# Attention values in runs of up to four steps, with strided sums of the weights on VectorE

## What is computed

```python
s = einsum('bqhd,bkhd->bhqk', q_nope, k_nope) + einsum('bqhr,bkr->bhqk', q_rope, kpe)
p = softmax(s * scale, axis=-1)
o = einsum('bhqk,bkhd->bqhd', p, v)
```

## Time and profile before

| | us |
|---|---|
| median of three runs | 3077.3 (3075.81 to 3077.61) |
| span of the profiled execution, first to last instruction | 3073.1 |
| the profiled execution's own time beside its span | not listed apart; the median lies 4.2 above the span |
| attention, first score to last convolution tile | about 930 to 1836 |

### The profile page before, as it was taken

One profiled execution on the slowest core, in us unless ns is written; L12 is line 12 of the kernel. 1 busy time (PEld: TensorE's weight loads), 2 busy tenths in 40 slices (PEclk: granted clock), 3 DMA queues, 4 the chain that ended last, 5 costly groups with the idle time before them and its releaser, 6 DMA issues. The chain is left out here.

```text
span 3073.1 us, 42659 instructions
## 1 busy us (share of the span) xinstructions
PE 2897.7 (94%) x16288; PEld 2284.8 (74%) x16288; DVE 1953.7 (64%) x2559; ACT 1085.5 (35%) x1723; POOL 1070.6 (35%) x693
## 2 busy tenths in 40 slices
PE   6999999999889999999999999989977999999993
PEld 3888888888676666666666667878856888888882
DVE  5418292829438888888888866555575555555555
ACT  5311111111344444444444443223432333434344
POOL 1000000000105343443433554522136766666652
PEclk9999999999898999999999999999988999999996
DMA  6213222211441110110110117675534666666657
GB/s 235 102 50 108 79 102 79 100 73 61 171 152 32 27 33 7 32 33 7 34 26 6 55 53 226 182 248 179 168 135 140 199 205 200 194 204 211 205 186 291
DMA packets 139518, 371.25 MB, mean 121 GB/s; under 512 B 20886, under 2 KB 47996, under 8 KB 129116
## 3 DMA queue, kind: packets, MB, share of 16 engines
q1 hardware_dynamic: 99756, 266.55, 26.0%
q0 software_dynamic: 24048, 74.72, 8.6%
q10 hardware_dynamic: 15552, 27.79, 2.6%
HBM read 266.07 MB, written 102.89 MB: 120 GB/s over the span
## 5 line engine op out<-in xcount | busy, mean ns | idle before, releaser
L1209 ACT ACTIVATE at_w<-banks 128x512 f32<-128x512 f32 (+1 forms) x592 | 347.6, 591 | 463.6 <-PE banks L1316 407.9
L1432 DVE TENSOR_REDUCE at_mpart<-banks 128x1 f32<-128x512 f32 (+1 forms) x584 | 373.7, 682 | 136.5 <-PE banks L1343 136.5
L1288 POOL TENSOR_TENSOR at_part<-at_part,at_w 128x512 f32<-128x512 f32 x224 | 297.6, 1329 | 327.2 <-ACT at_w L1209 323.9
L2705 POOL TENSOR_TENSOR late<-moe_raw_gu,late 128x2048 fp32r<-128x2048 f32 x62 | 287.2, 4633 | 121.6 <-ACT late L2770 121.3
L536 DVE SCALAR_TENSOR_TENSOR fr_r<-fr_r,fr_dw 128x2334 f32<-128x2334 f32 x120 | 318.0, 2650 | 3.9
L393 PE MATMUL fr_po<-hT_hi,fr_w_hi 128*128 128x512 f32 (+1 forms) x800 | 297.3, 372 | 3.0 <-PE fr_po L393 1.8
L393 PE MATMUL fr_po<-hT_hi,fr_w_lo 128*128 128x512 f32 (+1 forms) x800 | 294.9, 369 | 0.0
L393 PE MATMUL fr_po<-hT_lo,fr_w_hi 128*128 128x512 f32 (+1 forms) x800 | 294.9, 369 | 0.0
L1354 PE MATMUL banks<-at_w,V 128*64 128x256 f32 (+1 forms) x2368 | 283.0, 381 | 0.0
L2897 DVE TENSOR_TENSOR late<-raw,late 128x1024 fp32r<-128x1024 f32 x64 | 192.0, 3001 | 100.8 <-ACT late L2809 100.8
L1458 DVE TENSOR_TENSOR at_part<-at_part,at_w 128x512 f32<-128x512 f32 x224 | 231.5, 1033 | 13.0
(11 more groups left out here) (404 smaller groups left out, 6295.6 us busy)
## 6 DMA issues: line engine op xcount, KB each, us to landing
moe_raw_gu<-w_gate_up SPq DMA_DIRECT2D x62, 1024.0 KB, 4.8
raw<-w_down SPq DMA_DIRECT2D x64, 512.0 KB, 4.0
fr_wm<-w_ada_rows POOLq DMA_DIRECT2D x32, 512.0 KB, 4.3
gates_scratch<-fr_r ACTq DMA_DIRECT2D x64, 256.0 KB, 2.0
mx_gates<-gates_scratch SPq DMA_DIRECT2D x64, 256.0 KB, 3.1
fr_raw<-w_in SPq DMA_DIRECT2D x28, 512.0 KB, 5.5
fr_r<-x POOLq DMA_DIRECT2D x18, 512.0 KB, 5.5
raw<-mixed_scratch SPq DMA_DIRECT2D x9, 1024.0 KB, 6.0
```

The source lines that it names most:

```text
L1209: act.activation(w[:, g % NW, k, 0:n], sc[:, (2 * g + k) % SCB, 0:n], ACT.Exp, scale=SM_SCALE).then_inc(exp_done, 1)
L1288: pool.tensor_tensor(part[:, j % 2, 1, 0:n], before, w[:, g % NW, 1, 0:n], ALU.add).then_inc(add_p, 1)
L1432: dve.tensor_reduce(mpart[:, s, tiles, c // 2], bank, AX.X, ALU.max).then_inc(red_done, 1)
L2705: pool.tensor_tensor(gu_lo[:, slot], raw_gu[:, slot], gu_hi[:, slot].bitcast(F32), ALU.subtract).then_inc(glo_done, 1)
```

## The change

Steps are put into groups by a list of the last step of each (`ENDS`): 0 to 2, 3 to 6, 7 to 10, 11 to 14, 15 to 17, 18 to 21, 22 to 25, 26 to 29, 30 to 33, 34 to 35, and the prompt's step 36 together with 0 to 2 of the next head. For each group TensorE does the scores and maxima of all its steps, then the sums of blocks that ended in the group before, then the values of the same group in one run.

`part` goes; `w` has six slots in its place, the outer two of which hold the partial sums. The steps of a group lie in the inner four so that the steps of one block, with the partial sum so far at their side, are neighbours. VectorE sums them in one `tensor_reduce` that reads the slots with the slot as the innermost dimension (neighbouring elements of a sum are 2 x 512 floats, 4096 bytes, apart) and writes the partial sum on the other side or, for the first and last run of a block, on the block's own side. GpSimd still adds one step at a time. The prompt's sum is made by TensorE from its two tiles with ones, in a bank of the maxima's ring, and no engine adds or copies for it. ScalarE takes finished blocks out after the exponentials of the group that follows. The convolution's pieces keep their step numbers.

```diff
+    ENDS = (2, 6, 10, 14, 17, 21, 25, 29, 33, 35)
...
+    GROUPS = [[]]
     for g in range(G):
-        ADDS.append(ADDS[-1] + joins(g))
+        GROUPS[-1].append(g)
+        if g % PER in ENDS and g + 1 < G:
+            GROUPS.append([])
...
-        w = p.sb("w", [P, NW, 2, BLK])
-        part = p.sb("part", [P, 2, 2, BLK])
+        w = p.sb("w", [P, NW + 2, 2, BLK])
...
-                        if g >= NW:
-                            act.wait_ge(pv_mm, g - NW + 1)
-                            act.wait_ge((add_d, add_p)[k], adds_over(g - NW))
+                        if USED_BY[g] is not None:
+                            act.wait_ge(pv_mm, USED_BY[g] + 1)
+                            if whole(block_of(USED_BY[g])):
+                                act.wait_ge((add_d, add_p)[k], (D_ADDS, P_ADDS)[k][USED_BY[g]])
...
+                    for k in range(2 if own else 0):
+                        for half in range(2):
+                            mm = pe.matmul(acc_of(j)[half * DV:(half + 1) * DV, 256:256 + n], ones[:],
+                                           w[:, SLOT[g], k, half * n:(half + 1) * n],
+                                           start=(k == 0), stop=(k == 1), skip_group_check=True)
...
-                for g in range(0, G, 2):
-                    scores(g)
...
-                    if g:
-                        values(g - 2)
-                        values(g - 1)
...
+                for n, group in enumerate(GROUPS):
+                    for g in group:
+                        scores(g)
+                        for m in maxima_at(g):
                             max_products(m)
-                    if g:
-                        for j in turns(g + LA):
+                        for j in turns_at(g):
                             turn_max(j)
...
+                    for j in summed(n):
+                        sum_up(j)
+                    for g in group:
+                        values(g)
...
-                def add(g):
...
-                        dve.tensor_tensor(part[:, j % 2, 0, 0:n], before, w[:, g % NW, 0, 0:n], ALU.add).then_inc(add_d, 1)
+                def add(j, members):
+                    own = 0 if j % BH % 2 == 0 else NW + 1
+                    other_side = NW + 1 - own
+                    lo, hi = SLOT[members[0]], SLOT[members[-1]]
+                    out = other_side if third(j, members) == 1 else own
+                    dve.wait_ge(exp_done, 2 * members[-1] + 1)
+                    if third(j, members):
+                        dve.wait_ge(add_d, D_ADDS[members[-1]] - 1)
+                        lo, hi = min(lo, NW + 1 - out), max(hi, NW + 1 - out)
+                    if third(j, members) == 1 and number(j):
+                        dve.wait_ge(sum_mm, number(j))
+                    dve.tensor_reduce(w[:, out, 0], w[:, lo:hi + 1, 0].rearrange("p s n -> p n s"), AX.X, ALU.add).then_inc(add_d, 1)
...
+                    for j, members in RUNS[n]:
+                        add(j, members)
+                        if last_of(j) in members:
+                            join(j)
```

More of the change, by code:

```diff
@@ L1000, in turns, with summed, alone, unit_entries @@
         return [j for j in range(1, H * BH) if last_of(j) in (m - 2, m - 1)]
[L1002 to L1006, removed]
+    def summed(n):
+        return [j for j, members in (RUNS[n - 1] if n else ()) if last_of(j) in members]
+    def alone(n):
+        return [g for g in GROUPS[n] if not whole(block_of(g))]
+    def unit_entries(m):
+        return [("unit", UNITS[m] + half) for half in range(halves_of(m))] if m < G else []
+    def maxima_at(g):
+        if g < 2:
+            return (FIRST_MAX + 2 * g, FIRST_MAX + 2 * g + 1)
+        return (g + LA,) if g + LA < G else ()
+    def turns_at(g):
+        return turns(g + LA) if g > 1 and g % 2 == 0 else []
+    RING = [entry for m in range(FIRST_MAX) for entry in unit_entries(m)] + [("turn", 0)]
+    for n, group in enumerate(GROUPS):
+        for g in group:
+            RING += [entry for m in maxima_at(g) for entry in unit_entries(m)] + [("turn", j) for j in turns_at(g)]
+        RING += [("own", block_of(g)) for g in alone(n) if g + 1 < G]
     BANK, BEFORE, LAST_IN = {}, {}, {}
@@ L1082, in bank_of, with acc_of, part @@
             return mx[:, at] if at < MXB else sc[:, at - MXB]
+        def acc_of(j):
+            if whole(j) or last_of(j) + 1 == G:
+                return acc[:, number(j) % 2]
+            return bank_of(("own", j))
+        def part(j, k):
+            return w[:, 0 if j % BH % 2 == 0 else NW + 1, k]
         def paired(m):
@@ L1275, in _ @@
                         fold_conv(g % PER // 2 - 7)
-                    if not joins(g):
+                    j = block_of(g)
+                    if not whole(j) or c == 0:
                         continue
-                    j, n = block_of(g), BLOCKS[b][1]
                     pool.wait_ge(exp_done, 2 * g + 2)
[L1280 to L1288, removed]
+                    if c > 1:
+                        pool.wait_ge(add_p, P_ADDS[g] - 1)
+                    elif before(j) >= 0:
+                        pool.wait_ge(sum_mm, number(before(j)) + 1)
+                    so_far = part(j, 1) if c > 1 else w[:, SLOT[g - 1], 1]
+                    pool.tensor_tensor(part(j, 1), so_far, w[:, SLOT[g], 1], ALU.add).then_inc(add_p, 1)
                 for k in range(CT):
@@ L1322, in bank_free @@
                         kind, n = BEFORE[entry]
-                        pe.wait_ge(red_done if kind == "unit" else row_done, n + 1)
+                        pe.wait_ge({"unit": red_done, "turn": row_done, "own": o_done}[kind], n + 1)
                 def turn_max(j):
@@ L1410, in _ @@
-                values(G - 2)
-                values(G - 1)
-                for j in ended(G - 2) + ended(G):
-                    sum_up(j)
+                        if g == G - PER + TAIL:
+                            pe.wait_ge(conv_const, 2)
+                            pe.wait_ge(c_summed, 3)
+                            pe.wait_ge(row_done, H * BH)
+                            pe.matmul(mean, mean_w, sq[:, 0], start=True, stop=True).then_inc(mean_mm, 1)
+                        if g == G - PER + TAIL + 6:
+                            pe.wait_ge(sq_summed, 3)
+                            pe.matmul(var, mean_w, sq[:, 0], start=True, stop=True).then_inc(var_mm, 1)
```

175 lines of the change are left out of this document (77 added, 98 removed).

## The result

The change makes the kernel slightly slower: 3085.65 us (median of six runs, 3083.49 to 3088.74) against 3076.97 (six runs, 3075.81 to 3077.97), a ratio of 1.003 with a 95% interval of 1.002 to 1.004. The forecast was 3059, so it missed by 27 us and had the wrong sign; 3085.65 lies inside the range, near its upper end. The profiled execution took 3083.59 us, its span is 3081.8.

The account below looks back on a forecast made before the run. TensorE's own stream was taken to bound attention. Terms -25.2 + 1.7 + 0 + 5.4 = -18.1 us took the span from 3073.1 to 3055.0, and with 4.2 for the median 3059 us; range 3050 to 3090.

Parts of the forecast that it names:

- I take 1.04: VectorE's strided sum: 1.04 ns an element at a 4096-byte step, the rate of a contiguous reduction.
- sums by one strided operation: VectorE in attention: 96 reductions replace 256 additions, each ending before TensorE needs the next exponentials; cost 0.
- Bounds and range: Strided sum's rate: lower bound 1.04 ns an element, upper 2.02; whole kernel's range 3050 to 3090 us.
- the limits: Where a late sum stalls TensorE: fourth score tile's exponential by 13.3 us, fourth maxima unit's bank by 14.9.
- The hop is charged: Rival at VectorE's group sum: the wide step slows it and stalls TensorE; +67 us, 3126 us, chance 0.24.
- Fewer runs: TensorE in attention: 74 fewer runs of values at 0.34 us of joints each, -25.2 us.
- Joints not all saved: Rival at TensorE's joints: some gaps remain however values are grouped, a run worth 0.19 us; 3070 us, chance 0.07.
- Sum late though the rate holds: Rival at VectorE's group sum: uncounted waits add 1 us in three groups a head; 3072 us, chance 0.08.
- Prompt by products: TensorE's prompt sum: two more products with ones per head, 0.22 us in each of 8 heads, +1.7 us.
- Order at the end: Last head: the convolution norm's chain through root and silu ends later, delaying the last products; +5.4 us.
- faster: Whole kernel: outcome below 3071 us, faster by over 0.2%, given chance 0.66.

Follow-up runs that it names:

- experiment 1: The kernel before, with the values of each pair of steps split into two runs of one step, 147 more runs: 3129.9 us, ratio 1.017.
- experiment 5: The changed kernel, with strided sums over at most three places and the remaining places added by plain additions: 3074.04 us, ratio 0.9981 to the kernel before.
- experiment 2: The changed kernel, with every strided sum cut to at most three slots, so weights are missing from the divisor: 3062.43 us, ratio 0.995 to the kernel before.
- experiments 3 to 7: Changed kernel with: appended probe sums (3141.16 us); additions by step (3072.86); three-place sums plus additions (3074.04); the last two with earlier norm (3067.11, 3077.02).

## Why the prediction was wrong

**The step that failed** is "I take 1.04", in the part on sums by one strided operation: the cost of an element at a step of 4096 bytes. It measured 1.78 in the sums over four and five slots, which hold 224 of the 352 slots, and 1.06 to 1.14 in the others. The row that I took for the nearest, a copy of 16 elements, was too short and on the wrong side (a write) to carry that choice, and no row of a reduction over four places existed.

- *Bounds and range.* Both ends, 1.04 and 2.02, were kept, and 1.78 lies between them; so the time fell into the range though the likeliest value did not. The prediction put the stall's beginning at 1.4 and the loss of all gain at 1.6. At 1.78 in 48 sums, 1.1 in 48, all the gain and 9 us more were gone: the limits were about right, and both were met, the score banks (12.8 us of weight loads waiting for ScalarE) and the maxima banks behind the splits (10.4 us).
- *The hop is charged*, the slower rival with chance 0.24, is what happened, in its place and with its waits, but only from four places on. By its worst rate it gave 3126. The sentence on the Trainium skill (Vector Engine (DVE) Microarchitecture Reference, section 5.2, 1.73 ns a column for a source that hops 4 KiB at every element) gave 3087. For four to eight places the traces agree with that figure, with 1.68 to 1.83; for three they do not, with 1.15, and the exception that the section names, two regions at full rate, covers only the two.
- *Fewer runs*, -25.2: right. The waits called issue halved, and a run measured 0.342 us at one clock (experiment 1) against 0.34.
- *Joints not all saved*: refuted by the same run.
- *Sum late though the rate holds*: not seen. In experiment 5 the sums over five slots take 3.4 us with their additions, longer than the forecast's 2.8, and stand in the same place; the inner stretch still came to -22.1 of about -21.
- *Prompt by products*, +1.7: not isolated; it is too small for the median.
- *Order at the end*, +5.4: the last product came 3.15 us later from the scores of step 26, where 1.8 and 0.2 for the last prompt's products were forecast. With the 2.6 that is 5.8, so the size was near. The mechanism was right in its first half only: the root's table loads hold up the exponentials, and TensorE with them (2.91 us). In the second half the prediction had the last products wait for silu, whose table load came at 35.5 us, 34 forecast. They did not wait for it: TensorE waited 3.23 us for VectorE's last join, which stands behind the norm's last step and the sum of the last steps. With short sums the same wait is 3.02 us. That the number came out is partly luck.

Summed up: +8.0 measured against -18.1, of which the sums' rate makes up the most. Cutting it out (experiment 2) brings -9.9 at the milestone and -14 in the median, and from the first score to the last convolution product -15.95 (883.38 against 899.33). One slip changes nothing: the chances of *faster* add up to 0.685 (0.61 and half of 0.15), where the prediction has 0.66.

## What to carry to other kernels

When an operation on a slower path replaces several, its cost is not its busy time but when it ends: one sum behind the last step of a group has to fit into the slack of one group, while the additions that it replaces were spread over it. Where no row shows an operation's access pattern at its real number of places and length, treat the rate as open; then the chance of the slow end should weigh as much as the gain that hangs on it. And before believing a few microseconds of a long kernel, split the time by milestones, and set them inside a stretch with one granted clock: here a later stage moved by 8 us by itself, and the first 25 us of attention by 2 and more with the clock.

## What the hardware showed that was not expected

- A strided sum on VectorE reads two or three places at 1.06 to 1.15 ns an element, and four to eight at 1.68 to 1.83, whatever the step from 2048 to 4112 bytes. Why the edge lies there was not tried.
- A tenth of a microsecond in the order in which VectorE and GpSimd start goes with 7 to 10 us over the experts: five of the ten profiles (experiments 3 to 7) took 757.5 to 760.5 us from routing to end, the others 750.1 to 751.1. Four of the five kernels have plain additions in place of the long sums, the fifth has the long sums; what brings it on stays open.
- The start of attention itself varied from 933.8 to 939.2 us between profiles, before any changed instruction of TensorE's ran. The granted clock came back to 1.00 between 942 and 955 us, so the mean over the 25 us from the first score was 0.67 to 0.83.
